# Rotary part of the full attention: cosine terms added by VectorE instead of by an identity product and ScalarE copies

## What is computed

```
def apply_rope(x, cos, sin):
    x1, x2 = jnp.split(xf, 2, axis=-1)
    return concat([x1 * c - x2 * s, x2 * c + x1 * s])

def mla_attention(q_lat, kv_lat, k_rope, ...):
    q = (rms_norm(q_lat, q_norm_g) @ w_uq).reshape(b, s, h, 96)
    q = concat([q[..., :64], apply_rope(q[..., 64:], cos, sin)])
    k_pe = apply_rope(k_rope[:, :, None, :], cos, sin)
    k = concat([k_nope, broadcast_to(k_pe, (b, s, h, 32))])
    ... softmax(q k / sqrt(96)) v, in four blocks of 128 queries
```

## Time and profile before

| | us |
|---|---|
| median of 3 runs | 1506.73 |
| lowest and highest | 1504.9 and 1507.6 |
| the profiled execution | 1507.82 |
| its span, first to last instruction | 1506.0 |
| PE busy | 1371.6 (91%) |
| DVE busy | 488.0 (32%) |
| ACT busy | 298.1 (20%) |
| mean granted clock of PE | 0.982 |

### The profile page before, as it was taken

How to read it: one execution, slowest core, us unless ns; L and a number is a source line. 1 busy time by engine, 2 the same in 40 slices (tenths; PEclk the granted TensorE clock), 3 DMA queues, 4 the chain that set the end, 5 groups by cost and what they waited for, 6 DMA issues and landing times.

```text
span 1506.0 us, 15278 instructions
## 1 busy us (share of the span) xinstructions
PE 1371.6 (91%) x6282; PEld 698.7 (46%) x6282; DVE 488.0 (32%) x909; ACT 298.1 (20%) x515; POOL 120.6 (8%) x100
## 2 busy tenths in 40 slices
PE   6999999899999999989689998999999999998883
PEld 5666578543333333323267575865333333333330
DVE  5774754411111111110459467361101111110105
ACT  2336630100000000000143547101000000000000
POOL 1330000000000000000153100000000000000004
PEclk9999999999999999999999999999999999999997
DMA  9200332999999999999940013269999999999991
GB/s 384 108 1 1 140 141 84 416 404 426 428 427 428 427 426 427 426 428 428 422 190 1 0 57 141 99 247 395 429 427 426 428 427 428 426 428 427 428 425 71
DMA packets 43396, 462.02 MB, mean 307 GB/s; under 512 B 7744, under 2 KB 8384, under 8 KB 14912
## 3 DMA queue, kind: packets, MB, share of 16 engines
q1 hardware_dynamic: 32832, 436.88, 69.0%
q0 software_dynamic: 3744, 13.63, 2.2%
q10 hardware_dynamic: 6752, 10.54, 2.0%
HBM read 450.55 MB, written 10.49 MB: 306 GB/s over the span
## 4 chain that ended last, share of the span: by engine, by line
PE 70%; DMA 17%; DVE 6%; issue 3%; ACT 2%; POOL 1%; SPq 0%; ACTq 0%; DVEq 0%; POOLq 0%
PE bank L876 20%; DMA ring<-w_moe 15%; PE bank L899 12%; PE bank L512 10%; PE bank L850 8%; PE bank L767 2%; PE bank L771 2%; PE bank L770 2%; PE bank L465 2%; PE bank L749 1%; PE bank L838 1%; PE bank L828 1%; PE bank L656 1%; PE bank L740 1%; DVE X L1425 1%
## 5 line engine op out<-in xcount | busy, mean ns | idle before, releaser
L876 PE MATMUL bank<-ring,work 128*64 128x512 f32 x1600 | 354.5, 594 | 21.3 <-DMA ring<-w_moe 11.0
L876 PEld LDWEIGHTS bank<-ring,work 128*64 128x64 f32 x1600 | 128.4, 137 | 222.7 <-issue 189.4
L899 PE MATMUL bank<-ring,w_up 128*64 128x512 f32 x864 | 194.2, 596 | 20.0 <-DMA ring<-w_moe 9.8
L1425 DVE TENSOR_TENSOR X<-X,bank 128x512 f32<-128x512 f32 x128 | 87.9, 687 | 305.8 <-PE bank L850 305.6
L1413 DVE TENSOR_TENSOR work<-work,bank 128x512 f32<-128x512 f32 x32 | 22.0, 687 | 437.2 <-PE bank L876 436.0
L850 PE MATMUL bank<-work,cst 128*128 128x512 f32 x256 | 125.5, 620 | 13.1 <-ACT work L1717 11.2
L899 PEld LDWEIGHTS bank<-ring,w_up 128*64 128x64 f32 x864 | 66.4, 137 | 137.0 <-issue 116.7
L876 PE MATMUL bank<-work 128*64 128x512 f32 x448 | 99.3, 592 | 1.5 <-issue 1.5
L512 PE MATMUL bank<-x_hi,w_hi 128*128 128x512 f32 x288 | 80.3, 424 | 8.0 <-ACT x_hi L1476 6.7
L850 PEld LDWEIGHTS bank<-work,cst 128*128 128x128 f32 x256 | 40.7, 188 | 98.5 <-DVE X L1425 45.0
L1076 DVE SCALAR_TENSOR_TENSOR bank<-X,par,bank 128x512 f32<-128x512 f32 x120 | 79.9, 750 | 0.9 <-DVE ring L1050 0.9
(11 more groups left out here) (214 smaller groups left out, 1491.6 us busy)
## 6 DMA issues: line engine op xcount, KB each, us to landing
ring<-w_moe SPq DMA_DIRECT2D x154, 2048.0 KB, 29.3
work<-w_moe SPq DMA_DIRECT2D x38, 2048.0 KB, 29.3
ring<-w_in SPq DMA_DIRECT2D x18, 1024.0 KB, 22.3
ring<-w_out SPq DMA_DIRECT2D x8, 1024.0 KB, 28.0
out<-X POOLq DMA_DIRECT2D x12, 512.0 KB, 5.7
X<-out ACTq DMA_DIRECT2D x2, 2048.0 KB, 7.8
work<-ln SPq DMA_DIRECT2D x4, 1024.0 KB, 20.7
x_rows<-X ACTq DMA_DIRECT2D x8, 512.0 KB, 2.8
```

The costliest lines, as they stand in the source:

```text
L876: ins = mm(B((kind, pair, n))[64 * e:64 * e + 64, :], xsT[:, k, 64 * e:64 * e + 64], w[:, e, n * 512:(n + 1) * 512], start=(k == 0), stop= ...
L899: ins = mm(B(("O", pair, n))[64 * e:64 * e + 64, :], hidT[:, k, 64 * e:64 * e + 64], w[:, i, e], start=(k == 0), stop=(k == KD - 1))
L1425: nc.vector.tensor_tensor(X[:, t, cols], X[:, t, cols], B(name)[:, :], ALU.add)\
```

## The change

PE no longer multiplies by the identity for `ropeK` and `ropeQ`: `roped` gets no cosine product there, and its bank holds the sine term alone. DVE adds the cosine product while it fills `Kh` and `Qh`: four additions for the key and four for the queries, 32x512 each, from the bank and `a_parts` into `ring`. They stand on DVE behind `turned_parts` and ahead of `d_max(0)`. The five ACT copies of a layer (one 32x2048, four 32x512) are gone.

```diff
@@ roped (PE) @@
                     before(pe, name, lay)
-                    mm(B(name)[rows, :], ident[rows, rows], cosines, start=True, stop=False)
-                    mm(B(name)[rows, :], turn[rows, rows], sines, start=False, stop=True)\
+                    if cosines is not None:
+                        mm(B(name)[rows, :], ident[rows, rows], cosines, start=True, stop=False)
+                    mm(B(name)[rows, :], turn[rows, rows], sines, start=(cosines is None), stop=True)\
                         .then_inc(fullsem(name), 1)
@@ PE's order @@
-                roped(("ropeK",), 4, rot_a, a_parts[r, 0], a_parts[r, 1], r)
+                roped(("ropeK",), 4, rot_a, None, a_parts[r, 1], r)
                 k_up(0)
-                roped(("ropeQ",), 5, rot_a, a_parts[:, 2], a_parts[:, 3])
+                roped(("ropeQ",), 5, rot_a, None, a_parts[:, 3])
@@ DVE's order @@
                 if lay > 0:
                     hold(consts_back, 16 * lay)
+
+                def turned_keys():
+                    full(v, ("ropeK",), lay)
+                    for h in range(MLA_H):
+                        ins = nc.vector.tensor_tensor(Kh[r, h, :], B(("ropeK",))[r, :], a_parts[r, 0], ALU.add)
+                    ins.then_inc(freesem(("ropeK",)), 1)
+
+                def turned_queries():
+                    full(v, ("ropeQ",), lay)
+                    for h in range(MLA_H):
+                        rows = slice(ROPE * h, ROPE * (h + 1))
+                        ins = nc.vector.tensor_tensor(Qh[r, h, :], B(("ropeQ",))[rows, :], a_parts[rows, 2], ALU.add)
+                    ins.then_inc(freesem(("ropeQ",)), 1)
+
+                turned_keys()
+                turned_queries()
                 d_max(0)
@@ ACT's order @@
-                copy_out(("ropeK",), Kh[r, :, :],
-                         B(("ropeK",))[r, :].unsqueeze(1).broadcast_to([ROPE, MLA_H, S]))
                 keys_out(0)
-                for h in range(MLA_H):
-                    copy_out(("ropeQ",), Qh[r, h, :], B(("ropeQ",))[ROPE * h:ROPE * (h + 1), :],
-                             frees=(h == MLA_H - 1))
                 d_exp(0)
```

## The result

| | before | after |
|---|---|---|
| median of 5 runs, us | 1506.73 | 1515.11 |
| lowest and highest | 1504.9 and 1507.6 | 1514.31 and 1519.16 |
| profiled execution and its span | 1507.82, 1506.0 | 1519.16, 1517.3 |
| mean granted clock of PE | 0.982 | 0.977 |
| ratio, 95% interval | | 1.0063 (1.0052 to 1.0075) |

The change is slower. By the ratio it costs 9.5 us (7.8 to 11.3), where 7.1 had been forecast; 1506.73 x 1.0063 = 1516.2 lies 0.4 us above the upper end of the range (1509.3 to 1515.8). It is a narrow miss: the median itself, 1515.11, lies inside the range, and the interval of the ratio, 1514.6 to 1518.0, reaches into it. Which term was off is therefore read from the traces, not from this distance. The profiled execution is the slowest of the five, so what its trace shows is at the upper side of the cost.

The account below looks back on a forecast made before the run. PE was taken to bound the kernel, with 70% of the chain of waits. A 4.1 us delay from the bank 2 wait plus 3.0 of slow clock gave 7.1 us on the median 1506.73: 1513.8, range 1509.3 to 1515.8.

Parts of the forecast that it names:

- What bounds, and what ACT's copies are worth: PE bounds the stretch to SC_C; two identity products save 1.72 us per layer, ACT's five copies nothing by themselves.
- The price of an addition: On DVE: 0.61 us start to start on the same partitions, 0.72 on others, 5.4 us until d_max(0) starts.
- The wait on bank 2: PE waits ahead of SD 3 until DVE's late d_max(0) reads SD 0; SC_C starts 2.05 us later per layer.
- The delay reaches the end: Later waits keep their distance from PE and expert weights are released by it, so 4.1 us carries over in full.
- The clock falls in both layers: About 3.4 us of PE idle time drops its clock to 1.2 GHz behind the wait; forecast case, chance 0.55.
- The price of the slow clock: Behind the wait on PE: 1.5 us taken per layer, 3.0 in two, between 0 and 1.7 per layer.
- cost by partitions: Rival: a 32-partition DVE addition costs a quarter of 0.69 us, all eight 1.4; 1504.3 us, chance 0.07.
- absorbed in the experts' stage: Rival: the weight stream there starts independently of PE, so a late PE only waits less; 1506.7 us, chance 0.09.
- going on: Rival: PE passes the waiting SD 3 and continues with SC_C, gaining 3.4 us; given no chance of its own.
- the case of one layer with a full clock: Rival: same bank 2 wait, clock falls in one layer, about 1512.3 us; chance 0.29 together with falling in none.
- The time of 1504.3 that stood for "faster": Rival of cheap DVE additions: gain of 1.72 - 0.5 us per layer, from 1506.7 less 2.4; chance 0.07.

Follow-up runs that it names:

- e7: Changed kernel with d_max(0) cut in two around the additions and ropeK in bank 7 instead of 4: median 1503.47 us, ratio 0.9979.
- e1: Changed kernel with score result SD 3 in bank 6 instead of bank 2, DVE's order kept: 1504.57 us, ratio 0.9988.
- e2: Changed kernel with the reads of SD 0 and SD 1 put ahead of DVE's eight additions, banks unchanged: 1504.3 us, ratio 0.9982.
- e3: Changed kernel with three useless identity matmuls on PE ahead of SD 3, filling the wait on bank 2: 1511.89 us, ratio 1.0031.
- e8: Changed kernel run again without alteration, to see the length of the slow clock: ratio 1.0066 to the kernel before, runs 1514.42 to 1518.57 us.
- e9: Changed kernel with one useless identity matmul on PE ahead of SD 3, the wait on bank 2 kept: 1514.31 us, ratio 1.0054.
- e4: Changed kernel with PE's identity products kept, so DVE's eight additions become eight copies: median 1519.71 us, ratio 1.0082.
- e5: Changed kernel with all four query additions reading rows 64 to 95, the same partitions as the key additions: ratio 1.0060 to the kernel before.
- e6: Changed kernel with SD 3 in bank 6 and ropeK in bank 7 instead of 4: ratio 0.9985 to the kernel before.
- e10: Changed kernel with only the key's additions on DVE, the queries as in the kernel before: 1505.06 us, ratio 0.9991.

## Why the prediction was right in kind and short in size

- **What bounds, and what ACT's copies are worth.** Right. ACT's 8.3 us less show nowhere: where the new waits are gone (e7), a layer is 1.71 to 1.73 us shorter up to `var`, which is the two identity products (1.72 forecast) and no more.
- **The price of an addition.** Right. Forecast 0.61 and 0.72 from start to start; 0.60 and 0.70 measured, and `d_max(0)` at 8.35 us after `mean` where 115.4 - 107.03 = 8.4 was forecast. Taking the upper bound for the five instructions on other partitions was right.
- **The wait on bank 2.** Right, in place and size. `SD` 3 starts 8.84 after `mean` (forecast 8.9). With the clock still full `SC_C` starts at 9.46, 2.16 later than before, where 2.05 was forecast; `SD` 3 alone takes 0.63 to `SC_C`, as long as the pair, and not the 0.42 assumed. e1 and e2 show it to be the cause: take it away and the loss is gone.
- **The delay reaches the end.** Right. It is carried through the next 83.9 us without a change, and what the two layers lose is what the program loses, within 1.1 us. The maxima are later than forecast (2.3 us instead of 1.6 in layer 0, by the starts of L1190 and L1189, 10.71 and 8.37 after `mean`), which costs nothing: from `k_up(1)` to `var` it is 3.42 us, 3.41 in the kernel before.
- **The clock falls in both layers.** Right. e3 shows that the slow clock is caused by the idle time and has a price of its own.
- **The price of the slow clock.** Wrong: this is the term that was sized too small. With the measured wait, 2 x 2.16, and the 3.0 us taken for the clock the sum would be 7.3, well inside the range. The step was "up to 3.41 / 2 = 1.7 us if PE is busy in all of it", from the one slow stretch of the earlier trace rows, with 1.7 per layer as the upper bound. Stretches of twice that length occur as often in the five traces, and cost 2.8 to 3.1. The mean of the ten is (5 x 1.57 + 5 x 2.92) / 10 = 2.2 per layer, so the sum should have been 2 x (2.1 + 2.2) = 8.6 with 2 x (2.6 + 3.1) = 11.4 as its end. In the changed kernel's own four stretches (the profile after, and e8) the price was 3.14, 2.76, 1.59 and 2.99, on average 2.6, where 1.5 had been taken; 2 x (2.16 + 2.62) = 9.6 agrees with the 9.5 and 9.9 of the ratios. The trace of the kernel before had a warning, in two windows of the routing stages that the prediction did not look at:

```profile
263.87:270.70 6.83, 5.11 (x9) 2.30 (x9) 6.11 (x21) 1.54 (x2) 0.00 (x0) 0.51 1.01 425
1001.00:1007.57 6.57, 5.01 (x8) 2.08 (x8) 5.88 (x22) 1.54 (x2) 0.00 (x0) 0.50 0.98 418
```

- **The range.** Its ends don't follow from the prediction's own terms: the least loss that it counts, 2.8 us, gives 1509.5 and not 1509.3, and the most, 5.2 + 2 x 1.7 = 8.6, gives 1515.3 and not 1515.8. The ratio's 1516.2 lies outside either.
- **The rivals.** None of them came. An addition did not cost by partitions (0.68 us for 32 of them), nothing was absorbed in the experts' stage, PE stopped at `SD` 3 for 2.59 us instead of going on, and the case of one layer with a full clock was not seen in any of the five traces (after, e8, e9, e4, e5) that keep the wait and leave PE idle in it. The time of 1504.3 that stood for "faster" was only 2.4 us from no change, less than the 3.0 that the prediction itself took to be discernible.

What stays open: what decides whether the clock stays down for 3.4 or for 6.8 us, and how short a gap can be before it stops falling. e9 only shows that 1.54 us, behind 0.53 and some light matmuls, is still enough.

## What to carry to other kernels

An engine that is idle for 5.7 us is not free for 5.3 us of work: ask what it gave back before that idle time began. Here DVE's early read of a score result freed a bank which the bottleneck wanted soon after, and work put ahead of that read turned a saving of 3.4 us into a loss of 9.5; the same work put behind it keeps most of the saving (e2), and all of it with `ropeK` in a bank of its own (e7). Where a new wait leaves TensorE idle for one or two microseconds, count the slow clock behind it as a term of its own, and let its range reach to the price of the longer slow stretches in the trace, not of the nearest alone. What counts of a stretch is the part in which TensorE has work: the one of 10.2 us in the kernel before, from 748.6, holds only 3.9 us of it.

## What the runs showed of the hardware

- The slow clock behind a gap has no fixed length: 3.4 or 6.8 us for the same program at the same place (once and three times in the changed kernel, five times each in the ten cases of four kernels), at a cost of 1.6 or 2.9 us where PE has dense work. That is of the size of the wait itself, 2.2 us.
- The idle place at 62 to 65 us, 2.30 to 2.45 us long in every kernel, took the clock down in the profiles of before, e4, e5, e6, e7, e8 and e9 (`mean` of layer 0 then starts at 106.8 to 107.1), and not in those of after, e1, e2, e3 and e10 (`mean` at 105.3 to 105.4). So the same gap costs about 1.7 us in some executions and nothing in others, and its length doesn't decide it: 2.30 us took the clock down in e7 and not in e10, 2.45 us in e6 and not in e2.
- 1.54 us of idle time, behind 0.53 a little earlier, was enough for it, less than the 2.39 us of the only case in the middle of full work before; filling the whole gap with three matmuls whose result is thrown away won about 5 us over two layers. What a single one won (e9, +8.1 by the ratio against +9.5 and +9.9) the times don't tell from nothing.
- On DVE, a 32x512 copy out of a bank and an addition of a second operand out of SBUF take the same time (2.50 us for four), and changing the partitions from one instruction to the next costs 0.10 us each.
